# The causal mask of the diagonal score blocks, added by VectorE in the score bank instead of by a matmul

## The reference, cut to what matters

```python
s = jnp.einsum('bhqd,bhkd->bhqk', qb, k_all, ...) * scale
s = s + (Fqb[..., :, None] - F[..., None, :])        # forget gate: differences of a running sum
s = jnp.where(k_pos[None, :] <= qpb[:, None], s, -jnp.inf)   # causal mask
p = jax.nn.softmax(s, axis=-1)
return jnp.einsum('bhqk,bhkd->bhqd', p.astype(v_all.dtype), v_all)
```

## Time and profile before

| | us |
|---|---|
| median of 3 runs | 1898.44 (1896.52 to 1899.95) |
| the profiled execution, its own time | 1898.12 |
| its span on the slowest core (core 3) | 1896.6 |
| spans of the eight cores | 1893.5 to 1896.6 |
| PE busy (matmuls) | 1805.8, 95% |
| DVE busy | 764.0, 40% |
| ACT busy | 768.2, 41% |
| attention stage, from its first S to the output projection | 627.0 to 1314.5 |

### The profile page before, as it was taken

One profiled execution on the slowest core, in us unless ns is written; L12 is line 12 of the kernel. 1 busy time (PEld: TensorE's weight loads), 2 busy tenths in 40 slices (PEclk: granted clock), 3 DMA queues, 4 the chain that ended last, 5 costly groups with the idle time before them and its releaser, 6 DMA issues.

```text
span 1896.6 us, 35591 instructions; the slowest of 8 cores (1893.5 to 1896.6 us)
## 1 busy us (share of the span) xinstructions
PE 1805.8 (95%) x13360; PEld 962.7 (51%) x13360; DVE 764.0 (40%) x1405; ACT 768.2 (41%) x1492; POOL 136.1 (7%) x223
## 2 busy tenths in 40 slices
PE   3799999999998799999999999999999999999997
PEld 1245545554444465656565656665444444544443
DVE  1343233212466355545555555554642223322255
ACT  2463100111465566666565666665751110011132
POOL 2002000110005200000000000000000000000000
PEclk9899999999999899999999999999999999999999
DMA  9703603895127231323133322333232210422013
GB/s 177 195 4 60 104 1 58 142 159 82 56 101 156 58 82 36 83 35 83 35 84 52 88 51 66 68 115 79 79 60 42 34 29 1 78 34 41 10 67 123
DMA packets 42319, 137.92 MB, mean 73 GB/s; under 512 B 5497, under 2 KB 7913, under 8 KB 39049
## 3 DMA queue, kind: packets, MB, share of 16 engines
q0 software_dynamic: 25392, 81.03, 26.2%
q1 hardware_dynamic: 16760, 54.62, 8.1%
HBM read 180.18 MB, written 36.22 MB: 114 GB/s over the span
## 4 chain that ended last, share of the span: by engine, by line
PE 89%; DMA 4%; DVE 3%; issue 2%; ACT 1%; POOL 1%; DVEq 0%; ACTq 0%; POOLq 0%; SPq 0%
PE pb L463 85%; PE pb L461 4%; DMA RG<-w_ada 2%; DVE tw L639 1%; DMA RX<-xT 1%; DMA fd<-RX 1%; DVE RX L690 1%; PE pb L1269 0%; DVE RX L651 0%; ACT RG L473 0%; ACT tw L473 0%; POOL RX L551 0%; DMA RX<-fd 0%; DVE RG L676 0%; POOL RX L548 0%
## 5 line engine op out<-in xcount | busy, mean ns | idle before, releaser
L463 PE MATMUL pb<-H,wsall 128*128 128x512 bf16 (+1 forms) x5760 | 1151.7, 348 | 22.9 <-ACT H L473 9.6
L463 PEld LDWEIGHTS pb<-H,wsall 128*128 128x128 bf16 x5760 | 509.6, 98 | 517.7 <-issue 41.1
L473 ACT ACTIVATE tw<-pb 128x512 bf16<-128x512 f32 (+3 forms) x320 | 169.3, 533 | 652.3 <-PE pb L463 643.0
L473 ACT ACTIVATE RG<-pb 128x512 bf16<-128x512 f32 (+3 forms) x688 | 345.1, 532 | 179.9 <-PE pb L463 152.8
L463 PE MATMUL pb<-RG,wsall 128*128 128x512 bf16 (+1 forms) x2080 | 387.6, 348 | 2.2 <-DVE RX L690 1.8
L676 DVE TENSOR_TENSOR RG<-pb,tw 128x512 bf16<-128x512 f32 (+1 forms) x218 | 132.8, 611 | 477.1 <-PE pb L463 434.6
L463 PEld LDWEIGHTS pb<-RG,wsall 128*128 128x128 bf16 x2080 | 186.7, 98 | 200.7 <-issue 5.3
L463 PE MATMUL pb<-RX 68*128 68x512 bf16 (+3 forms) x640 | 215.3, 349 | 10.0 <-DMA RX<-fd 10.0
L461 PEld LDWEIGHTS pb<-RX,RG 128*128 128x128 bf16 x2176 | 139.2, 97 | 107.6 <-issue 6.7
L690 DVE SCALAR_TENSOR_TENSOR RX<-pb,DER,RX 128x512 f32<-128x512 f32 (+1 forms) x192 | 112.5, 595 | 187.6 <-PE pb L463 182.0
L461 PE MATMUL pb<-RX,RG 128*128 128x65 bf16 x2176 | 169.7, 193 | 2.6 <-ACT RG L473 2.2
(11 more groups left out here) (108 smaller groups left out, 707.4 us busy)
## 6 DMA issues: line engine op xcount, KB each, us to landing
wsall<-w_in POOLq DMA_DIRECT2D x32, 512.0 KB, 6.8
wsall<-w_ada POOLq DMA_DIRECT2D x28, 512.0 KB, 12.4
wsall<-w1i POOLq DMA_DIRECT2D x22, 512.0 KB, 18.2
wsall<-w2i POOLq DMA_DIRECT2D x22, 512.0 KB, 9.8
RX<-xT SPq DMA_DIRECT2D x4, 2048.0 KB
xs<-RX SPq DMA_DIRECT2D x4, 2048.0 KB
kT<-RX SPq DMA_DIRECT2D x32, 256.0 KB
vo<-RX SPq DMA_DIRECT2D x32, 256.0 KB
```

Of the source, the lines that this page charges most:

```text
L463: ins = e.matmul(o, lhsT=l, rhs=r, start=st, stop=sp)
L473: return P.op("scalar", lambda e: e.activation(out=out, in_=in_, func=func, **kw), reads=reads, writes=writes)
```

## The change

The mask matmul goes. S is now a single matmul. In a diagonal step, E first emits a `tensor_tensor` on VectorE, which adds `maskneg` to the 128 diagonal columns in the score bank itself, in place; the exponential then reads the bank as before. Since the bank is exclusive, the exponential waits for VectorE and VectorE for S.

```diff
                 def S(i=i, r=r, lo=lo, box=box):
                     b = box["b"] = nxt_of("s", S_BANKS)
                     items = [(PB[b][:, lo:512], ka[0:68, hh, i * 128:(i + 1) * 128],
-                              qa[0:68, hh, q0 + lo:q0 + 512], True, r < 0)]
-                    if r >= 0:
-                        items.append((PB[b][:, lo:lo + 128], ident_bf[:], maskneg[:], False, True))
+                              qa[0:68, hh, q0 + lo:q0 + 512], True, True)]
                     mm(items, [B_k[st_][hh][i // 4], B_krow[st_], B_kone[st_], B_q[st_][hh][qb], B_qrow[st_],
                                B_qone[st_], B_const], [PBB[b]])
 
-                def E(lo=lo, box=box):
+                def E(r=r, lo=lo, box=box):
                     p = box["p"] = rot["pt"] % 4
                     rot["pt"] += 1
+                    if r >= 0:
+                        dg = PB[box["b"]][:, lo:lo + 128]
+                        vec(lambda e: e.tensor_tensor(out=dg, in0=dg, in1=maskneg[:], op=ALU.add),
+                            [PBB[box["b"]], B_const], [PBB[box["b"]]])
                     act(PT[p][:, lo:512], PB[box["b"]][:, lo:512], AF.Exp, [PBB[box["b"]]], [B_pt[p]])
```

## The result

The changed kernel takes 1938.9 us at the median (1937.96 to 1939.82; here and below, executions in which one die ran slower than the other are left out, and with the one of them the median is 1939.38). The ratio to the kernel before is 1.0207, with a 95% interval of 1.0193 to 1.0222: some 40 us slower. The forecast was 1952 us, 54 us slower. Direction and mechanism were right; the stalls (time in which PE stands because of the additions) were sized some 30% too large: 63 us forecast, 48 to 49 found.

The account below looks back on a forecast made before the run. PE's in-order queue was taken to bound the stage. 1898.1 - 14.6 (masks) + 63.4 (stalls) + 5 (clock) = 1951.9, forecast as 1952 us, 2.8% slower; range 1915 to 1990 us.

Parts of the forecast that it names:

- The mask term: PE's full queue in the attention stage: 256 mask matmuls gone at 0.057 us each, 14.6 us gained.
- The mask isn't on PE's path: Rival: PE's next matmul waits for something else, so removing masks gains nothing; 1967 us, no separate chance given.
- It balances: Rival: PE makes up most stalls, leaving about what the masks cost; 1898 us, chance 0.05.
- The stalls: PE waiting before V because additions queue behind other VectorE operations: 63.4 us, 53.6 in pairs 0 to 6.
- the walk: Tracing additions through VectorE's queue, quad by quad, with trace times and PE's other work unmoved; gave 63.4 us.
- Pair 7: Last head pair, without projections: shorter steps cover less of V's wait, so 9.8 us of stalls.
- The clock: PE's clock dropping after long gaps: 26 stalls over 1 us, one in nine costing 1.7 us, 5 us together.
- the clock falls with nearly every long stall: Rival: PE's clock loss becomes some 40 us instead of 5; 1987 us, chance 0.09.
- VectorE's busy time: Sign on VectorE: 256 additions of about 0.29 us raise its busy time by 75 us, to some 839.
- It hides: Rival: VectorE's additions fit within PE's two steps of other work, leaving only the 14.6 us gain; 1884 us, chance 0.06.
- The forms of the signs: Signs expected in the profile after, such as V's waits for ScalarE rising from 2.2 us to some 60.
- PE's busy share: Sign in the stage's middle stretches: PE's busy share falls from 99% to about 91 to 93%.

Follow-up runs that it names:

- ahead of the readings: Changed kernel with S and E of a step emitted before that step's side-bank readings on VectorE; 1937.7 us, ratio 1.0201.
- spread taps: Changed kernel with the convolution's three tap operations emitted over three steps instead of at once, all 256 additions kept; 1931.6 and 1932.5 us.
- three steps ahead: Changed kernel with S and E emitted three steps ahead of V instead of two, still over three score banks; 1938.4 us, ratio 1.0204.
- 105 additions: Against the kernel before: VectorE adds the mask at 105 places in pairs 0 to 6, all other masks stay matmuls; 1900.8 us, ratio 1.0008.

## Why the prediction was right, and where it was off

**The mask term** (14.6 us): right. It measures 13.6 us, 11 to 16, with nothing else changed but the scale in the diagonal exponentials. "The mask isn't on PE's path" falls with it: the path is PE's, and what leaves it is gained. "It balances" falls by the time itself, 40 us from it.

**The stalls** (63.4 us): the mis-sized term. The profiled executions differ by 1938.94 - 1898.1 = 40.8 us. With the masks' 13.6 to 14.6 us added, stalls and clock are some 55 us; without 6 for the clock, stalls are 48 to 49. Pairs 0 to 6 have 38 to 39 of them against 53.6 walked. Comparing the starts of V in the two traces, quad by quad, with the masks that went until there added (us):

| quad | walked | measured |
|---|---|---|
| (3,1), r = 2 and 3 | 1.67 + 0.58 | 1.45 + 0.5 |
| (0,1) | 1.0 | 0.5 |
| (1,0) | 0.8 | 0.4 |
| (1,1), r = 1 and 3 | 1.19 + 0.57 | 1.01 + 0.19 |
| (2,0) | 1.2 | 1.0 |
| (2,1) | 0.65 | 0.25 |
| (3,0) | 0 | 0.06 |
| sum | 7.66 | 5.36 |

Each of the stalls walked is there, in its place, and 0.1 to 0.5 too long. Two causes are seen in rows. The step of the walk that took VectorE's queue as a sum of durations overcounts, since neighbours overlap: by 0.09 for an addition behind L1160, 0.09 between two additions, 0.08 behind L1167; and ScalarE follows by 0.10 instead of 0.14. Over one to five links that makes 0.1 to 0.5. And the short stalls at the end of a chain, r = 3 of (1,1), (0,1), (2,1), are differences of two longer times, so that this error takes half of them or more. For (0,1), (1,0) and (2,1) I have the sum and not each link, so how their error is split is open.

**Pair 7** (9.8 us): a little low. It takes 12.2 us more; with its masks (1.8) added and two drops of the clock (3.4) taken off, 10.6 us of stalls are left. The run with additions in pair 7 alone has the same gaps of 2.27, 1.4 and 2.42 us and is 14 us slower. (1,0), walked at 2.75, shows 2.27 in its bracket and was too long like the rest; but two gaps close to the end, 1.32 and 0.96, lie ahead of the last transposes, where nothing of the next pair fills PE, and I had walked (3,1) at 1.4 in all.

**The clock** (5 us): about 6 in the end, with four further drops of up to 1.7 us, but the size was luck. The term took 26 stalls over 1 us and one drop in nine. By the bracket, as the nine were counted, V has 12 gaps over 1 us, and the four new drops follow four of them: half as many gaps, three times as likely. The rival "the clock falls with nearly every long stall" is wrong: of seven equal gaps at the joints, four left it at 1.00.

**VectorE's busy time** (75 us more, measured 57): the length of one was right, 293 ns, but 256 of them are busy for 68.2 us, since those in a row overlap; the rest of the difference I put down to overlap with other neighbours. It cost nothing either way.

**"It hides"**: wrong as a whole, right in single quads. Its bound of 0.23 us per quad isn't met: 49 us over 64 quads is 0.77. The additions placed only where the trace showed room gave nothing measurable. Three edits moved the order about (ahead of the readings, spread taps, three steps ahead); each moved stalls to another step or to S, and the best of them gained 7 of the 40 us. Of all runs only the one without a mask is measurably faster than the kernel before. Not tried: VectorE's long operations cut into short ones, or the mask on an engine with a shorter queue.

**The forms of the signs**: PE's waits by the bracketed rows, 37 us, were forecast at 60. That miss is larger than the stalls' own error, for a reason in how the view is read. A bracket counts from the modelled end of the matmul before, and that end is 0.16 us late for what can follow it: four of 128x512 take 1.03 us, a single one 0.38, so they start (1.03 - 0.38) / 3 = 0.217 apart. V has 56 bracketed gaps where it had 13, and 43 x 0.16 = 7 us more are in no bracket. 37.0 - 2.2 + 7 = 42 of the 48 to 49 us. The rest I put down to short waits: the shortest brackets in these rows are 0.15, so that a wait of up to 0.3 us can have none, as with 105 additions, where pairs lost 15 masks and gained no time. PE's busy share, 94 to 96% for the forecast 91 to 93, is in part the smaller stalls and in part this: busy time too counts to the modelled end.

## What to carry to other kernels

An instruction taken from the engine that bounds and put on a half-idle one in the path that feeds the first was priced here by the queue ahead of it, not by its length: 0.29 us of work made PE stand for up to 2.4 us, and stalls and clock cost four times what the masks had. Look first at which operations stand ahead of it when its input is ready, and at how much other work the bounding engine has until it needs the result; the step with the least cover decides, and moving the order about mostly passed the wait on. A walk by rows found the places; it was some 0.1 us too long per link. To size what was lost, compare starts of the same instruction in both traces, not brackets.

## What the runs showed of the hardware

- Two additions of 128x128 in score banks start 0.20 us apart, though each takes 0.29 (x2 takes 0.49). Neighbours on VectorE overlap by up to 0.09 us.
- Gaps of the same length on PE don't lower its clock alike. On the core shown, 1.15 us did at three of seven joints, 2.27 us in pair 7 did not, and 2.42 us did. All eight cores of that execution have these gaps: a drop followed 14 of 56 at the joints, four of eight of 2.27 us, and all eight of 2.42 us. Where it fell, the granted clock was 0.66 over 5 us, 1.7 us lost.
- 256 matmuls of 128 columns inside a full PE queue are worth 13.6 us, 53 ns each, a quarter of the 221 ns that a single one takes.
